# One split of the k/v weights and four k/v products block by block, in a transformer block pair on one core

## The reference, cut to what matters

```python
mod   = silu(c)     @ w_mod + b_mod          # sh1, sc1, g1, sh2, sc2, g2
mod_c = silu(c_ctx) @ w_mod + b_mod          # csh1, csc1, ...
hc = rmsnorm(ctx, norm1_g) * (1 + csc1) + csh1     # 256 tokens
k_c, v_c = split(hc @ w_in[:, 1024:1536])
hx = rmsnorm(x, norm1_g) * (1 + sc1) + sh1         # 512 tokens
q, k, v, u, b, c, ... = split(hx @ w_in)
q, k = rope(q), rope(k)
o = window_attention(q, k, v, k_c, v_c, sink)      # 16 heads, 4 key heads
y = short_conv(u, b, c)
```

## Time and profile before

| | us |
|---|---|
| runs | 2195.53, 2191.94, 2187.08; median 2191.94 |
| the profiled execution | 2191.43 |
| its span, first to last instruction | 2189.7 |
| TensorE busy | 1945.9 (89%) |
| VectorE busy | 972.6 (44%) |
| ScalarE busy | 636.7 (29%) |
| GpSimd busy | 111.4 (5%) |
| mean granted TensorE clock | 0.933 of 2.4 GHz |

### The profile page before, as it was taken

The page is one execution under the profiler, slowest core; times in us unless marked ns, Lnnn a source line. Parts: engine busy times, 40 slices in busy tenths (PEclk is TensorE's granted clock), DMA queues, the critical chain, the costliest instruction groups (busy, mean ns, idle before and its releaser), DMA issues.

```text
span 2189.7 us, 22924 instructions
## 1 busy us (share of the span) xinstructions
PE 1945.9 (89%) x9497; PEld 1394.4 (64%) x9497; DVE 972.6 (44%) x1589; ACT 636.7 (29%) x1090; POOL 111.4 (5%) x91
## 2 busy tenths in 40 slices
PE   5779999999997788889988859899898889999997
PEld 3667777778875443333433329789676668888886
DVE  3667767742544312121112164421645446534544
ACT  3444444542332110000100023321454424323322
POOL 0210100000000000000000020000302200000000
PEclk8889999999999899889898969899899899999998
DMA  9223233252342598989989903242211233133221
GB/s 303 97 68 126 79 105 125 78 173 97 101 174 77 215 409 351 388 326 367 386 327 380 394 27 104 68 163 72 77 39 58 77 115 97 60 104 115 73 92 39
DMA packets 203130, 357.15 MB, mean 163 GB/s; under 512 B 7090, under 2 KB 150546, under 8 KB 202258
## 3 DMA queue, kind: packets, MB, share of 16 engines
q1 hardware_dynamic: 198480, 337.74, 42.6%
q10 hardware_dynamic: 4258, 17.65, 2.2%
q0 software_dynamic: 288, 0.30, 0.1%
HBM read 347.57 MB, written 8.39 MB: 163 GB/s over the span
## 4 chain that ended last, share of the span: by engine, by line
PE 74%; DVE 11%; DMA 5%; ACT 4%; issue 2%; POOL 2%; SPq 0%; DVEq 0%; ACTq 0%
PE ps L432 72%; PE ps L435 3%; DMA ring<-in_w_exp_up 2%; DVE X L1629 2%; POOL tb L2415 2%; DMA rx<-in_w_exp_up 2%; ACT M L1038 1%; DMA ring<-in_w_mod 1%; DVE tb L1620 1%; DVE wsp1l L1620 1%; ACT k2h L1038 1%; DVE wsp0l L1620 1%; DVE onesrow L1629 1%; ACT tb L1038 0%; DVE small L1851 0%
## 5 line engine op out<-in xcount | busy, mean ns | idle before, releaser
L432 PE MATMUL ps<-H,wsq0h 128*128 128x512 f32 x704 | 224.4, 401 | 18.5 <-POOL H L2415 15.9
L432 PE MATMUL ps<-H,wsp0h 128*128 128x512 f32 (+1 forms) x624 | 201.1, 405 | 21.3 <-POOL H L2415 11.5
L432 PE MATMUL ps<-H,wsq1h 128*128 128x512 f32 x544 | 171.9, 398 | 6.6 <-DVE wsq1l L1620 6.6
L432 PEld LDWEIGHTS ps<-H,wsq0h 128*128 128x128 f32 x704 | 135.5, 194 | 50.3 <-issue 22.0
L432 PE MATMUL ps<-rx,XE 128*64 128x512 f32 x656 | 151.1, 593 | 1.7 <-DMA rx<-in_w_exp_up 1.2
L432 PEld LDWEIGHTS ps<-H,wsp0h 128*128 128x128 f32 x624 | 118.0, 197 | 49.8 <-issue 18.8
L432 PE MATMUL ps<-H,wsq0l 128*128 128x512 f32 x352 | 139.9, 397 | 0.0
L1620 DVE TENSOR_TENSOR wsq0l<-ring,wsq0h 128x1024 fp32r<-128x1024 f32 (+2 forms) x72 | 81.1, 1164 | 132.0 <-ACT wsq0h L1038 132.0
L432 PE MATMUL ps<-GT,Y 128*128 128x512 f32 x128 | 91.5, 811 | 49.0 <-DVE X L1629 45.2
L432 PE MATMUL ps<-H,wsp0l 128*128 128x512 f32 (+1 forms) x312 | 124.2, 398 | 0.0
L432 PEld LDWEIGHTS ps<-H,wsq1h 128*128 128x128 f32 x544 | 103.6, 192 | 29.3 <-issue 8.0
(11 more groups left out here) (309 smaller groups left out, 3769.0 us busy)
## 6 DMA issues: line engine op xcount, KB each, us to landing
rx<-in_w_exp_gate SPq DMA_DIRECT2D x45, 1024.0 KB, 12.4
rx<-in_w_exp_down SPq DMA_DIRECT2D x42, 1024.0 KB, 18.4
ring<-in_w_in SPq DMA_DIRECT2D x41, 1024.0 KB, 5.2
rx<-in_w_exp_up SPq DMA_DIRECT2D x37, 1024.0 KB, 8.8
ring<-in_w_exp_up SPq DMA_DIRECT2D x27, 1024.0 KB, 15.0
ring<-in_w_mod SPq DMA_DIRECT2D x24, 1024.0 KB, 7.0
ring<-in_w_exp_down SPq DMA_DIRECT2D x22, 1024.0 KB, 18.2
ring<-in_w_up SPq DMA_DIRECT2D x20, 1024.0 KB, 5.2
```

What stands on the lines that cost most here:

```text
L432: return pe.e.matmul(o, l, r, start=start, stop=stop, skip_group_check=True)
```

## The change

- Loads: x in four tiles and ctx in two go to SP's queue ahead of all weights. Then "k" (`ring0`), mod 4, mod 0, "v" (`ring1`), mod 5, 1, 6, 2, 7, 3; the mod pieces go through three places of their own (`md0` to `md2`, in `KR`) and `ring2`. The slabs "ck" and "cv" are gone. The cos and sin constants are loaded from ScalarE's queue after the split of "k".
- Norms: ScalarE squares the untransposed rows with a running sum (six instructions of 128x1024), one root and one reciprocal on 128x6; VectorE scales the identity by each of six columns, and a product with ones broadcasts them over the partitions.
- Mod pieces go in the order 4, 0, 5, 1, 6, 2, 7, 3, so that scale and shift of chunks 0 and 1 come first, and so on. The two scale tiles are made one with the output instruction.
- `keys_values(c)` does, for one chunk c of 128 features, all of ctx and x keys and values, into six PSUM banks that stay open over the eight blocks: 24 products of 256 columns and 6 of 512. Raw products of two mod pieces stand behind blocks 0, 2 and 4, their sums in the middle of blocks 1, 3 and 5.
- The tokens' low parts are all on VectorE; POOL's `left` is gone there, and x and ctx have tiles of their own. ScalarE writes the high part with the shift in one instruction everywhere.
- Keys: rotations have places of their own; low key parts are written to 64 partitions only, and the low score products take 64 rows (`qa[0:64]`): the product of two low parts is left out.
- ("q",0,0) is split into tiles of its own (`wsx`). Eight of the 124 units are done ahead of the loop, the other 116 are spread evenly over the 32 iterations, the last one included (`paced`).
- VectorE's and ScalarE's orders follow: behind the blocks VectorE has `lo("q",0,0)`, both rotations, `lo("q",0,1)`, the low ctx keys, the values, the low keys, `lo("conv",0,0)`.

```diff
-    for n in range(8):
-        piece(("mod", n), w_mod, 0, 8, 256 * n, split=False)
-    for key, c0 in (("ck", 1024), ("cv", 1280), ("k", 1024), ("v", 1280)):
-        piece(key, w_in, 0, 8, c0)
+    early = [4, 0, 5, 1, 6, 2, 7, 3]
+    early_places = [("md0", md[0]), ("md1", md[1]), ("md2", md[2]), ("ring2", ring[2])]
+    piece("k", w_in, 0, 8, 1024)
+    for j, n in enumerate(early):
+        piece(("mod", n), w_mod, 0, 8, 256 * n, 256, False, *early_places[j % 4])
+        if j == 1:
+            piece("v", w_in, 0, 8, 1280)
...
+    early_units, units = 8, 4 * 7 + 8 * 12
+    def paced(it, place):
+        upto = lambda k: (units - early_units) * k // 128
+        k = 4 * it + (0, 2, 3, 4)[place]
+        return upto(4 * it + (2, 3, 4)[place]) - upto(k)
...
 # TensorE
+        to_t("x", xtok, 4)
+        to_t("ctx", ctok, 2)
...
+        def norms():
...
+            mm(bank(b), onesrow[:, 0:P], diag[:, 256:768], True, True)...
+            mm(bank(c, 0, L), onesrow[:, 0:P], diag[:, 0:256], True, True)...
...
+        def keys_values(c, between=()):
+            first, last = c == 0, c == 7
+            (kh, kl), (vh, vl) = hi_lo(slabs["k"]), hi_lo(slabs["v"])
+            for part in range(2):
+                for name, th, tl, N in (("ctx", HCh, HCl, L), ("x", Hh, Hl, T)):
+                    pe.wait_ge(S["v_put" if part else "a_put"], (name, c))
...
+                    for m in range(2):
...
+                        if part == 0:
+                            mm(o, kh[:, c, w], th[:, c, :], first and (name == "x" or m == 0), False)
+                            mm(o, kl[:, c, w], th[:, c, :], False, False)
+                        else:
+                            i = mm(o, kh[:, c, w], tl[:, c, :], False, last)
...
+                    for n in range(N // P):
...
+                        if part == 0:
+                            mm(o, th[:, c, w], vh[:, c, :], first and n % 2 == 0, False)
+                            mm(o, th[:, c, w], vl[:, c, :], False, False)
+                        else:
+                            i = mm(o, tl[:, c, w], vh[:, c, :], False, last)
...
+                if part == 0:
+                    for f in between:
+                        f()
+        mod_raw(0)
+        norms()
+        mod_sum(0)
+        mod_raw(1)
+        mod_sum(1)
+        for c in range(8):
+            if c % 2:
...
+                    keys_values(c, [lambda: mod_sum(j), lambda: mod_sum(j + 1)])
...
+            else:
+                keys_values(c)
+                if c < 6:
+                    mod_raw(c + 2)
+                    mod_raw(c + 3)
...
-                mm(S0, qa, Kl[:, g, lo:hi], False, False)
+                mm(S0, qa[0:64], Kl[0:64, g, lo:hi], False, False)
...
 # VectorE
+        for c in range(0, 8, 2):
+            norm_c(c)
+            norm_x(c)
+            norm_c(c + 1)
+            if c == 0:
+                lo(slabs["v"])
+            left_c(c)
+            norm_x(c + 1)
+            left_x(c)
+            left_c(c + 1)
+            left_x(c + 1)
+            if c < 6:
+                for j in (c + 2, c + 3):
+                    mod_row(j)
+                for j in (c + 2, c + 3):
+                    mod_out(j)
...
+        lo(slabs["q", 0, 0])
         for m in range(2):
-            twice("ck", m, tb[:, 0:L], KCl, L)
+            rotate(("k", m), ("k", m), bank(m), kr[m], [("v_put", ("x", 7))])
+        lo(slabs["q", 0, 1])
...
+        lo(slabs["conv", 0, 0])
...
 # ScalarE
+        def put_first(name, c, o, h, shift):
+            ac_.wait_ge(S["v_put"], (name, c, "n"))
+            act(h, o, ACT.Identity, bias=shift[:, c:c + 1]).then_inc(*S["a_put"].tick((name, c)))
...
+        hi(slabs["q", 0, 1])
+        ac_.wait_ge(S["v_put"], ("x", 7))
+        ac_.wait_ge(S["pe_group"], ("ck", 1))
+        act(cs, bank(4), ACT.Copy).then_inc(*S["a_take"].tick("ck"))
...
+        act(ct[:, :], cs, ACT.Copy).then_inc(*S["a_rope"].tick(("ck", "t")))
+        twice("ck", 0, cs[:, 0:L], KCh)
+        hi(slabs["conv", 0, 0])
+        twice("ck", 1, cs[:, L:2 * L], KCh)
         for m in range(2):
             ac_.wait_ge(S["g_rope"], ("k", m))
...
+            act(kt[:, m * T:m * T + T], kr[m][:, 0:512], ACT.Copy)...
+            twice("k", m, kr[m][:, 0:512], Kh)
...
 # all three engines, ahead of the loop and in it
+        for _ in range(early_units):
+            next(more)
         for it in range(32):
             g, n = it // 8, it % 8
             soft(g, n)
-            next(more, None)
-            next(more, None)
+            for _ in range(paced(it, 0)):
+                next(more)
```

More of the change, by code:

```diff
@@ L522, in lin_n, with turn_vec @@
             final[key] = (key, len(toks) - 1)
[L526 to L531, removed]
+        turn["banks"] = [0, 1, 2, 3, 4, 5]
+        def turn_vec(key, src, n, frees, ready):
+            b = take(key, frees)
+            need(ready)
+            tr(bank(b, 0, n), src, ident[0:n, 0:n]).then_inc(*S["pe_turn"].tick(key))
@@ L532, in mod, with mod_raw @@
+        def mod_raw(j):
+            n, b = early[j], 6 + j % 2
             s = slabs["mod", n]
-            b = take(("mod", n), [("v_mod", (n, "out"))])
+            hold(b, [("v_mod", (n, "out"))])
             pe.wait_ge(S["a_take"], ("c", 1))
-            pe.wait_ge(S["v_set"], 3)
+            pe.wait_ge(S["v_set"], 2)
             pe.wait_ge(S[s.slot], s.key)
             for k2 in range(2):
-                for j in range(4):
-                    i = mm(ps[32 * j:32 * j + 2, b * 512:b * 512 + 256], cTv[:, 2 * j + k2, :], s.raw[:, 2 * j + k2, :],
+                for j4 in range(4):
+                    i = mm(ps[32 * j4:32 * j4 + 2, b * 512:b * 512 + 256], cTv[:, 2 * j4 + k2, :], s.raw[:, 2 * j4 + k2, :],
@@ L561, in tensor @@
[L561 to L583, removed]
@@ L660, in tensor @@
         free["scores"] = free[2] + free[3] + free[4]
+        turn["banks"] = [6, 7]
         for _ in fill(fills[0]):
@@ L668, in tensor @@
         more = beside()
+        for n in range(early_units):
+            if n == 4:
+                turn["banks"] = [0, 1]
+            next(more)
         scored = turned = None
@@ L683, in tensor @@
             scored = (g, n)
-            next(more, None)
+            for _ in range(paced(it, 2)):
+                next(more)
         for _ in more:
@@ L1682, in vector @@
                 cp(dst[:, c, :], bank(where.get((name, c), 0), 0, N)).then_inc(*S["v_turn"].tick((name, c)))
-            for c in range(8):
-                if c:
-                    v.wait_ge(S["a_norm"], (name, c))
-                    if c > 1:
-                        v.wait_ge(S["v_norm"], (name, c - 1))
-                    tt(sums, sums, tbv[c % 2][:, 0:N], ALU.add).then_inc(*S["v_norm"].tick((name, c)))
-                if c in mods:
-                    mod(mods[c])
-            if name == "ctx":
-                v.wait_ge(S["a_norm"], ("ctx", "root"))
-                v.e.reciprocal(sums, sums).then_inc(*S["v_norm"].tick(("ctx", "rs")))
@@ new lines, in vector, with mod_row @@
+        for i in range(6):
+            d = ts1(diag[:, i * P:(i + 1) * P], ident, rstd[:, i:i + 1], ALU.mult)
+        d.then_inc(*S["v_norm"].tick("diag"))
+        v.wait_ge(S["pe_turn"], "vec2")
+        cp(vt2[:, :], bank(where.get("vec2", 0), 0, 112)).then_inc(*S["v_turn"].tick("vec2"))
+        def mod_row(j):
+            n, b = early[j], 6 + j % 2
+            v.wait_ge(S["pe_mod"], (n, "raw"))
+            if j > 1:
+                v.wait_ge(S["pe_mod"], (early[j - 2], "sum"))
+            cp(mrows[j % 2][0:98, :], ps[0:98, b * 512:b * 512 + 256]).then_inc(*S["v_mod"].tick((n, "row")))
@@ new lines, in mod_out @@
+        def mod_out(j):
+            n, b = early[j], 6 + j % 2
+            v.wait_ge(S["pe_mod"], (n, "sum"))
+            v.wait_ge(S["v_mod"], "bias")
+            for h in range(2):
+                o = bank(b, 256 + 2 * h, 258 + 2 * h)
+                if n < 4:
+                    c = 2 * n + h
+                    i = ts1(modv[:, c, :], o, bmod[:, c:c + 1], ALU.add)
+                else:
+                    c = 2 * n + h - 8
+                    i = ts(gAv[:, c, :], o, bmod1[:, c:c + 1], n1g[:, c:c + 1], ALU.add, ALU.mult)
+            i.then_inc(*S["v_mod"].tick((n, "out")))
```

359 lines of the change are left out of this document (192 added, 167 removed).

## The result

The changed kernel takes **2219.0 us** (median of 4 runs, 2210.09 to 2221.93), the kernel before 2193.74 beside it on the same chip: a ratio of 1.0112, 95% interval 1.0073 to 1.0151. It is 25 us **slower**, where 24 us less were forecast. The profiled execution of after took 2221.93 us, 3 us over its median.

The account below looks back on a forecast made before the run. TensorE bounds the attention loop, nothing bounds the stretch ahead of it. From 2191.4 us: -16.9 for earlier second scores, -9.5 for seven more units, +2.5 for the clock's fall gives 2167.5 us; range 2151 to 2182.

Parts of the forecast that it names:

- Part 1: Loads and transposes at the kernel's start: tokens land first, and the transposes end at 21 us.
- Part 2: Norms and first two mod pieces: second sum at 31 us, or 28 if raw products run at 2.4 GHz; 31 kept.
- Part 3: Eight key and value blocks from 33 to 84 us: 13 us a pair, 0.7 idle; slow first pair, 16.
- T: Moment when all four key and value products end, after the eight blocks: forecast at 84 us.
- Part 4: From the blocks' end to the second attention scores: 37 us, reaching them at 121 us with 15 units done.
- The 128 low score products with 64 rows for 128: Attention loop: equal width in columns, so costed at nothing; at most -8.6 us if rows counted.
- The thinner spacing: Attention loop: 3.6 fill units an iteration for 4, costed at nothing because VectorE has 80 us to spare.
- -9.5: Term in us for seven more fill units done by the second scores.
- rival B: Attention loop: VectorE's queue or waits for `mod_sums` make units ahead worth nothing; the 9.5 us fall away, 2177 us; chance 0.16.
- A: Start all covered: second scores at 111 us, no fall of the clock, 2155 us; chance 0.12.
- C: Clock stays down in the blocks: 21.2 us a pair, second scores at 149, 2193 us; chance 0.08.
- D: Seam of each block pair: TensorE stops 3 us, clock falls, 24.2 us a pair, 2204.5 us total; chance 0.05.

Follow-up runs that it names:

- full_rows_old_pace: The changed kernel with low score products on 128 rows, no unit ahead of the loop and four in every iteration: 2167.58 us, ratio 0.9904 to the kernel before.
- half_rows_alone: The kernel before with only the low score products on 64 rows: 2218.11 us, ratio 1.0135 to the kernel before.
- full_rows: The changed kernel with the low score products over 128 rows again: 2183.27 us, ratio 0.9968 to the kernel before.
- eight_ahead_old_pace: The changed kernel with 128-row low score products, eight units ahead of the loop, then four an iteration until gone: 2197.52 us, ratio 1.0049 to the kernel before.
- none_ahead_even: The changed kernel with 128-row low score products, nothing ahead of the loop, 124 units spread evenly: 2188.74 us, ratio 0.9982 to the kernel before.

## Why the prediction was wrong

**Part 1** holds: transposes end at 22.7 for 21. **Part 2** holds with the lower value that I named and didn't take: 28.05. The raw products right behind the transposes took 1.04 us at 22.67, the duration of the 2.4 GHz level in the earlier trace rows. The granted clock was 1.00 from the start to 30 us, though transposes were all that TensorE did up to 22.7: in before it rose during them, here it held. So the Trainium skill (TensorE: Matmul & The Clock Gate, Part 4: PE-mode transpose) is at odds with this trace too, and the 3 us that I kept for unseen waits were not needed.

**Part 3** holds and was cautious: T = 77.87 for 84, 3 us of it from part 2. The first pair began slowly, as it said, at a clock of 0.53 up to 36 us. The 0.7 us idle at each pair and the extra in "I take 13" did not come: 40.00 us busy of 40.

**Part 4** holds nearly to the digit: T + 15.5, T + 23.5, T + 35.6 for T + 15.4, T + 22 to 24, T + 37. The clock fell ahead of them and behind them too, and lasted longer than the 4 to 5 us that were forecast for +2.5: from 113.48 it stayed at 1.2 GHz until 122.6, 9.1 us, some 4.5 us lost. Counting from events works: full_rows_old_pace has its second scores at 112.1 with eight units done, as before had at 137.95. 2191.4 - 25.8 is 2165.6; it took 2167.6.

**The sum** is where it failed, in two of its terms that both stood at nothing.

"The 128 low score products with 64 rows for 128 are as wide in columns: nothing; at most half of 64 x 0.27 us, -8.6": **this step failed, and cost 28 to 36 us** (half_rows_alone against before 28; after 2219.0 against full_rows 2183.3, 32 by the ratios). The products by themselves do cost the same. What was missed is their neighbours: each stands between 128-row products, and its weights were not loaded beside them (306.63 above). The bound had a gain on one side and on the other nothing, though no row of before has a 64-row product and no reason spoke against a loss. The Trainium skill (TensorE: Matmul & The Clock Gate, Part 2, Step-by-step: what each phase is for) says that a weight load is pulled ahead of running products when the row groups don't conflict or when it goes to the background weight buffer. By the rows above, loads of 128 rows do run beside 128-row products, and loads of another row count start only near their end; the page gives no price, the runs give 0.154 us a change.

"The thinner spacing (3.6 units an iteration for 4) I cost at nothing, since VectorE has 80 us to spare": **this step failed, and cost some 16 us against the old pace** (full_rows over full_rows_old_pace), together with the "-9.5" for seven more units done. 80 us to spare over 330 say nothing of one iteration, in which VectorE's work comes in lumps and in order. In the loop of after TensorE waits for a split six times, 2.5 to 3.9 us each, where none in before is over 2.2, and the clock falls behind them more often and for longer. Units ahead are worth nothing here: none 2167.6, four 2164.8, eight 2172.1 at best. That is what rival B is named for, though not its 2177; its mechanism, a wait around `mod_sums`, was real at the old pace (eight_ahead_old_pace), on VectorE and not on TensorE, and small at the change's own.

With the second scores at 113.48 my own sum would give 2191.4 - 24.5 - 9.5 + 2.5 = 2159.9. Its loop is then 315.0 us (322.0 - 9.5 + 2.5), and 373.0 were measured: 58 us over, of which 39 are the changes of row count and the rest, 19, waits for late splits and the clock behind them (20 by the account above: 6 idle and 16 of clock, less the 2.5 forecast). With 4 us in the rest of the kernel that is 2221.9, and the profiled execution took 2221.93. The marker "the loop from there takes longer than 314 us" was the one that broke, by 59 us; the mark "0.50 in the pairs" broke for the first pair only. **A**'s timing of the start came nearly true, though not its clock without a fall; **C** and **D** did not: from 40 us on the clock stayed at 1.00 in the blocks, and no seam showed. The slower side did come, by a mechanism that none of the rivals had.

## What to carry to other kernels

An edit costed at nothing because "it has the same width" needs a loss side when the trace has no such instruction: ask what it stands between. Products of 64 and of 128 rows belong in runs of their own kind, or all on 128 rows. In a loop paced by hand, keep the filling work in whole units at fixed places of the iteration: an engine's total slack doesn't tell whether a lump of its work, or a wait that it meets in order, lands ahead of something needed at once.

## What the runs showed of the hardware

A change between 64-row and 128-row products costs TensorE 0.154 us here (1.23 us for eight), shown by no idle time on PE at all but only by longer products (391 ns for 295) and by the time at which the weight load starts. Waits of 3.70 us (none_ahead_even, 170.02) and of 2.17 us (full_rows_old_pace, 163.15) were both followed by the 1.2 GHz level: 0.50 from 170 to 172 and from 163.2 to 166.5. Yet after a wait of 3.10 us behind the transposes of after the raw products still ran at 1.04 us. So the length of the wait alone did not decide it.
